# Shifting where four SBUF buffers start, by multiples of 32 bytes, in a two-block transformer kernel

## The reference

```python
h = jnp.einsum('bsd,de->bse', x, w_in[l])            # 1024 -> the widths of all branches
...
mix = jnp.einsum('bsd,de->bse', merged, w_out[l])
x = _layer_norm(DEEPNORM_ALPHA * x + mix, ln1_g[l], ln1_b[l])
u = jnp.einsum('bsd,df->bsf', x, w_ffn_in[l])        # 1024 -> 2 * 2816
ffn = jnp.einsum('bsf,fd->bsd', jax.nn.silu(u_gate) * u_up, w_ffn_out[l])
x = _layer_norm(DEEPNORM_ALPHA * x + ffn, ln2_g[l], ln2_b[l])
```

## Time and profile before

| | us |
|---|---|
| median of 3 runs | 2028.66 (2027.19 to 2028.98) |
| profiled execution: its own time | 2028.55 |
| profiled execution: span, first to last instruction | 2026.5 |

### The profile page before, as it was taken

How to read it: one execution, slowest core, us unless ns; L and a number is a source line. 1 busy time by engine, 2 the same in 40 slices (tenths; PEclk the granted TensorE clock), 3 DMA queues, 4 the chain that set the end, 5 groups by cost and what they waited for, 6 DMA issues and landing times.

```text
span 2026.5 us, 32504 instructions
## 1 busy us (share of the span) xinstructions
PE 2010.0 (99%) x14176; PEld 1835.6 (91%) x14176; DVE 1274.6 (63%) x1844; ACT 927.0 (46%) x1275; POOL 32.2 (2%) x56
## 2 busy tenths in 40 slices
PE   8999999999999999999999999999999999999998
PEld 7888999999887999999999989799999998979997
DVE  6566666555756665655665567765566556776555
ACT  4445444444545444544444454454444445445442
POOL 0000000000000000000000000000000000000000
PEclk9999999999999999999999999999999999999999
DMA  8544555666544555586556646458656664555663
GB/s 287 168 149 132 187 172 168 199 207 190 167 163 136 167 168 186 147 261 187 167 181 188 185 135 167 105 157 251 187 167 188 187 188 134 158 136 157 189 188 101
DMA packets 416133, 352.51 MB, mean 174 GB/s; under 512 B 28816, under 2 KB 361080, under 8 KB 415992
## 3 DMA queue, kind: packets, MB, share of 16 engines
q1 hardware_dynamic: 415992, 350.44, 57.3%
HBM read 349.36 MB, written 1.05 MB: 173 GB/s over the span
## 4 chain that ended last, share of the span: by engine, by line
PE 94%; DVE 3%; ACT 2%; issue 0%; DMA 0%; DVEq 0%; SPq 0%
PE ps L201 29%; PE ps L202 29%; PE ps L203 29%; PE ps L1446 2%; PE ps L1527 2%; PE ps L1565 1%; DVE hl L1990 1%; PE ps L1599 1%; ACT hl L1749 1%; DVE er L2157 0%; DVE small L2116 0%; ACT er L1841 0%; PE ps L1637 0%; DVE er L2114 0%; PE ps L1570 0%
## 5 line engine op out<-in xcount | busy, mean ns | idle before, releaser
L1990 DVE TENSOR_TENSOR hl<-raw,hl 128x1024 fp32r<-128x1024 f32 (+2 forms) x555 | 756.3, 1393 | 393.5 <-ACT hl L1749 392.5
L201 PE MATMUL ps<-xt,hl 128*128 128x256 f32 (+1 forms) x2672 | 753.5, 282 | 0.0
L202 PE MATMUL ps<-xt,hl 128*128 128x256 f32 (+1 forms) x2672 | 746.0, 279 | 0.0
L203 PE MATMUL ps<-xt,hl 128*128 128x256 f32 (+1 forms) x2672 | 745.5, 279 | 0.0
L1749 ACT ACTIVATE hl<-raw 128x2048 fp32r<-128x2048 f32 (+1 forms) x323 | 612.8, 1899 | 183.6 <-PE ps L203 169.4
L201 PEld LDWEIGHTS ps<-xt,hl 128*128 128x128 f32 (+1 forms) x2672 | 501.0, 187 | 4.7 <-issue 1.5
L202 PEld LDWEIGHTS ps<-xt,hl 128*128 128x128 f32 (+1 forms) x2672 | 500.9, 187 | 3.2
L203 PEld LDWEIGHTS ps<-xt,hl 128*128 128x128 f32 (+1 forms) x2672 | 500.8, 187 | 0.2
L201 PE MATMUL ps<-hl,o 128*128 128x512 f32 x656 | 261.9, 399 | 0.0
L203 PE MATMUL ps<-hl,o 128*128 128x512 f32 x656 | 259.4, 395 | 0.0
L202 PE MATMUL ps<-hl,o 128*128 128x512 f32 x656 | 259.4, 395 | 0.0
(11 more groups left out here) (202 smaller groups left out, 1605.8 us busy)
## 6 DMA issues: line engine op xcount, KB each, us to landing
raw<-in_w_in SPq DMA_DIRECT2D x83, 1024.0 KB, 5.1
raw<-in_w_ffn_in SPq DMA_DIRECT2D x88, 512.0 KB, 5.2
raw<-in_ffn_gate SPq DMA_DIRECT2D x88, 512.0 KB, 4.0
raw<-in_ffn_up SPq DMA_DIRECT2D x88, 512.0 KB, 5.3
raw<-in_ffn_down SPq DMA_DIRECT2D x44, 1024.0 KB, 5.0
raw<-in_w_ffn_out SPq DMA_DIRECT2D x22, 1024.0 KB, 5.0
raw<-in_w_out SPq DMA_DIRECT2D x12, 1024.0 KB, 5.1
raw<-in_w_branch_a SPq DMA_DIRECT2D x8, 1024.0 KB, 4.9
```

The source lines that it names most:

```text
L201: e.matmul(out, l[0], r[0], start=start, stop=False)
L202: e.matmul(out, l[0], r[1], start=False, stop=False)
L203: return e.matmul(out, l[1], r[0], start=False, stop=stop)
L1990: e.tensor_tensor(lo[:, c], m["raw"][:, k % NRAW, 0:n][:, c], hi[:, c].bitcast(F), ALU.subtract).then_inc(s.low.up(("low", k), *([("low", ...
```

## The change

Four small buffers that no instruction uses are put between the others: `apart0` (32 bytes per partition) ahead of `hl`, `apart1` (64) ahead of `xs`, `apart2` (96) ahead of `o1`, `apart3` (64) ahead of `o2`. They move the buffers behind them. The instructions, their order, their shapes and their waits are the same on every engine; only addresses differ.

```diff
         m = {
-            "raw": sb("raw", [128, NRAW, UNIT]), "hl": sb("hl", [128, NHL, 2, UNIT], R),
+            "raw": sb("raw", [128, NRAW, UNIT]), "apart0": sb("apart0", [128, 8]), "hl": sb("hl", [128, NHL, 2, UNIT], R),
             "const": sb("cst", [128, NCONST]), "maskb": sb("maskb", [128, 3, 128], BF),
-            "x": sb("xs", [128, 2, D]), "xt": sb("xt", [128, 2, 8, S], R),
-            "o1": sb("o1", [128, 2, 8, S], R), "o2": sb("o2", [128, 2, 4, S], R), "gb": sb("gb", [128, 2, D]),
+            "apart1": sb("apart1", [128, 16]), "x": sb("xs", [128, 2, D]), "xt": sb("xt", [128, 2, 8, S], R),
+            "apart2": sb("apart2", [128, 24]), "o1": sb("o1", [128, 2, 8, S], R), "apart3": sb("apart3", [128, 16]), "o2": sb("o2", [128, 2, 4, S], R), "gb": sb("gb", [128, 2, D]),
```

## The result

The changed kernel takes 2043.61 us (median of 4 runs, 2042.84 to 2045.35) against 2028.43 us for the kernel before in the same comparison: a ratio of 1.0077, with a 95% interval of 1.0064 to 1.0089. It is 15.2 us slower, where 12.2 were forecast, and its time lies between the 2037 and 2045 us of the forecast. The profiled execution has a span of 2040.9 us, 14.4 more than before's.

The account below looks back on a forecast made before the run. The prediction took TensorE's matmul pace to bound the kernel. Its terms, 12.0 + 1.2 - 1.0, summed to +12.2 us, so about 2041 us, with a range of 2037 to 2045 us (8 in 10: 2027 to 2047).

Parts of the forecast that it names:

- What bounds the kernel: On TensorE, busy 99% of the span: the pace at which matmuls follow each other sets the end.
- Part 1: 256 columns of xt moving past stationary hl: 7968 matmuls, each 1.5 ns slower, +12.0 us.
- Part 2: o1 and o2 moving past stationary hl: 768 matmuls, each 1.5 ns slower, +1.2 us.
- Part 3: 256 columns of hl moving past xt: 672 matmuls go from 118.1 to 116.7 ns, -1.0 us.
- Part 4: 512 columns of hl moving: 3024 matmuls, load covered, no change; upper bounds 4.5 or 9 us, no gain.
- Parts 5 and 6: Residual matmuls and transposes, and VectorE and ScalarE operations on moved buffers: taken as nothing.
- The reason I gave: 256-column matmuls: a stationary operand off a 128-byte boundary touches a fifth piece, pushing its weight load past 5 ns of cover.
- Its signs: Right: xt past hl at 118.1 to 118.3 ns, hl past xt 116.7, 512 columns 233.2; wrong: 512 columns above 234.
- Places do nothing: All matmuls: the 1.4 ns comes from step kind or earlier work; time stays 2028.7 us; chance 0.15.
- the faster rival: 256-column matmuls: another pair of starts loses a conflict between the streams, 16.6 us off, 2012 us; chance 0.13.
- Slower by more: 512-column matmuls of hl pay too, 2045 to 2050 us; chance 0.10.
- Slower by less: 256-column stretches partly stay at 116.7 or settle at 117.7 ns, 2033 to 2037 us; chance 0.10.

Follow-up runs that it names:

- rows 128 further: Changed kernel with xs, xt, o1 and o2 a further 128 bytes on; 2040.03 us, 1.0058 of the kernel before.
- the isolated pairs: Kernel without the computation, only streaming fp32r matmuls over all 16 pairs of moving and stationary places modulo 128; 113.5 to 120.0 ns at 256 columns.
- The best layout: Kernel before with hl and o2 at 64, xt and o1 at 0 within 128 bytes; 2026.37 us, ratio 0.999.
- xt alone: Kernel before with only xt (and xs) moved, to place 0; 2043.45 us, 1.0078 of the kernel before.

## Why the prediction held, and where it didn't

The time came out inside the range, and by luck: the largest term was half of what it should have been, a term put at nothing made up for most of it, and the mechanism given for both was wrong.

**What bounds the kernel.** Right. The pace of the matmuls is the time; the whole 14.4 us of the span is in the split products, and the rest of the stream adds 0.0.

**Part 1, `xt` moving past `hl`: +12.0.** Measured +25.1. The sign is right, the size is half. I took the pair 0, 32 as "precisely the pair that runs at 118.1 before", and that was the step that failed: it was the same pair modulo 128 only. Modulo 256 the stretch that I timed has distance 160 - 128 = 32, and the changed main kind has 160 - 0 = 160. The prediction named the bits above 128 bytes as the one difference, and gave it no price. The version with rows 128 further has the distance 32 that I had in mind, and its main kind costs +12.3 us.

**Part 2, +1.2.** Measured -1.2 for `o1` and +0.6 for `o2`. The distances are 64, which can run at 113.4, and 0.

**Part 3, -1.0.** Measured -0.4 (118.3 to 117.6 ns on average; two of the twelve stretches stayed at 118.7).

**Part 4, 512 columns: nothing, and nothing from below.** Measured -9.8: -7.8 past `o2` (distance 0), -1.3 past `o1` (192), -0.7 past `xt` (96). This was the bound that I excluded, on the ground that the pace per column was the same at both places seen. They were two distances that happened to share a pace. Past `xt` the steady pace rose, from 233.2 to 234.3, and the -0.7 holds -1.4 from the start of the program. Parts 1 and 4 missed by 13 and 10 us with opposite signs, and so the sum came within 3.

**Parts 5 and 6, nothing.** Right: the rest of the stream adds 0.0, and the operations that write `hl` and `xt` stay at 1220 and 422 ns. The row of 693 ns stays too, but its buffers keep their places.

**The reason I gave.** A weight load that outgrows its cover because it begins off a 128-byte boundary: refuted, in all three of its claims. The stationary place alone doesn't set the pace, 512 columns with over 100 ns of cover react, and 120.0 is reached with both operands on the boundary.

**Its signs.** None of the pace signs of being right came: the main kind stands at 119.9 and not 118.1 to 118.3 (mean duration 282 and not 281), `hl` past `xt` with 256 columns at 117.3 and not 116.7, and 512 columns not at 233.2. One sign of being wrong came, 512 columns above 234 (past `xt`, 234.3). The total alone does not show this.

**The rivals.** "Places do nothing" fell with the isolated pairs, which have no other engine and no change of step, and differ by 6.5 ns. Its observation, that one pair of addresses has two paces, was right: 10 of the 106 main stretches before run at 117.8 to 117.9. The best layout missed its forecast for another reason first: it had been chosen modulo 128, and its main kind stood at distance 192 in place of 64. But 192 has two paces too (113.3 was seen in a stream), and there every stretch took the slow one. The mechanism of the faster rival, that how the two starts lie to each other counts, was the true one; only its sign was the other way, since the changed kernel's main distance is, with 0, the slowest of the multiples of 32. "Slower by more" had the sign of the 512-column part wrong: it gained. "Slower by less" did not occur: all 106 main stretches run at 119.8 to 120.1. The Trainium skill's rule that a weight load takes no bandwidth from the running matmul ("TensorE: Matmul & The Clock Gate", "Step-by-step: what each phase is for") would give the pace no reason to depend on where the stationary operand stands. These fp32r streams do not agree: 96 matmuls past a stationary operand at 0 take 120.0 ns each and past one at 64 take 113.5, with the moving operand in one place. That the load takes bandwidth is not shown by this, since distances still differ with 8 stationary columns.

So the cause of the changed time is shown: the distance between the two operands' starts, modulo 256 bytes, sets the pace. What stays open is what in the chip makes it so, why no stretch of 256-column matmuls came under 113.3 ns, even with 8 stationary columns, and what fixes which of two paces a stretch falls into.

## What to carry to other kernels

In a kernel bound by back-to-back fp32r matmuls, time the pace of each pair of operands from start times, and tabulate it against the distance of their starts modulo 256 bytes; a few spare bytes between buffers moved this one from 2043.6 to 1996.4 us. When a rule is drawn from one kind of step in a trace, list all in which the two cases differ, and give the leftover a price. Streaming kernels of 0.6 to 0.8 ms separated what whole-kernel variants only hinted at, but the first was tabulated modulo too short a period, and a stretch can have two paces, so a layout taken from one must be timed in place.

## What the runs showed of the hardware

- At a granted clock of 1.00 (2.4 GHz), the pace of fp32r matmuls with 128 stationary columns depends on the distance between stationary and moving start modulo 256 bytes: 113.3 to 120.0 ns at 256 columns, 226.7 to 234.3 at 512. Both operands moved on by the same amount keep the pace at distances 0, 32 and 224 (119.8 to 120.0, 118.3, 117.8); at 64 it was 113.5 once and 117.8 once.
- One distance can have two steady paces at 256 columns, held for whole stretches: 113.3 or 117.8 at 64 and at 192, 116.7 or 117.8 at 224, 118.5 to 118.8 or 120.0 at 128 (94 and 12 of the 106 main stretches of xt alone). In the two layers of the first stack the slow stretches are the same ones.
- The best distance depends on the moving columns: distance 0 is among the slowest at 256 and the fastest at 512.
- VectorE and ScalarE showed no such effect: over the nine layouts the operations that write `hl` (L1990, 1024 elements) and `xt` (L1805) took 1220 to 1221 ns and 422 to 425 ns.
